# A two-block transformer on one core: each weight unit's high part made by ScalarE in two instructions instead of one

## The chip, the cores and the metric

The kernel runs on one core of a Trainium2 chip, as one program and one launch. The metric is the device time of that program in microseconds, the median of several executions; lower is better. TensorE (PE) multiplies, VectorE (DVE), ScalarE (ACT) and GpSimd (POOL) work on whole tensors in SBUF and PSUM, SyncE (SP) issues the large transfers.

## The reference, cut to what matters

The input is 512 rows of 1024 values, in fp32. They pass through two layers of a first block and one layer of a second, and every matrix product of the reference is to be met at nearly fp32 accuracy.

```python
# first block, two layers
h = rmsnorm(x, g_mix[i])
mix, q_mem = mixer_a(h, ...)      # layer 0: indexer picks 128 keys a row, latent attention
mix, q_mem = mixer_b(h, ...)      # layer 1: causal window attention, window 128, with sinks
mem_o = memory_cross_attention(q_mem, mem_n, w_mem_kv[i])
x = x + concatenate([mix, mem_o]) @ w_out
a, b = split(rmsnorm(x, g_ffn[i]) @ w_up[i])                 # 1024 -> 2 x 2816
x = x + (silu(conv3(a)) * b) @ w_down[i]                     # 2816 -> 1024
# second block, one layer
sh1, sc1, gt1, sh2, sc2, gt2 = split(silu(c) @ w_mod + b_mod, 6)
h = rmsnorm(x, g_pre1) * (1 + sc1) + sh1
q, k, v, f, g_a, g_f = split_proj(h @ w_in)
attn = banded_window_attention_2(q, k, v, k_ctx, v_ctx, sink)
y = (sigmoid(g_a) * (attn @ w_pa) + sigmoid(g_f) * (fourier_mix(f) @ w_pf)) @ w_out
x = x + gt1 * rmsnorm(y, g_post1)
h2 = rmsnorm(x, g_pre2) * (1 + sc2) + sh2
x = x + gt2 * rmsnorm((silu(conv3(u)) * gate) @ w_down, g_post2)   # u, gate from h2 @ w_up
```

## The kernel before, in words

**Weights.** All weight matrices are laid out on the host as 173 units. A unit fills 128 partitions with `ph.size` columns of fp32: 2048 columns in 119 of them, 1408 in 32, 1280 in 16, 1536 in 4, 1024 in 2. The units form one stream of phases (`STREAM`, line 109), and each engine works through it in that order. The phases, with their units: `a_idx` 5, `a_in` 2, `memkv` 4, `a_q` 4, `uk`, `uv`, `a_out` 8 (the first layer's attention and its output), `up00` 22, `dn00` 8, `up01` 22, `dn01` 8 (its feed-forward part in two halves), `b_in` 7, `b_out` 8, `up10`, `dn10`, `up11`, `dn11` (the second layer), `ctx` 2, `c_in` 13, `merge` 4, `c_out` 4, `up20`, `dn200` to `dn203`, `up21`, `dn210` to `dn213` (the second block). The last unit of the program, of `dn213`, has 1536 columns.

**Each unit passes four engines.** SyncE's `load` (line 551) transfers it into one of two slots of `RAW`, which it may overwrite when the low part of the unit two before is written (`sp.wait_ge(lo_ready, ...)`). ScalarE's `hi_unit` (line 602) waits for the transfer and for TensorE to have done with the unit two before, and writes the value rounded to fp32r into a slot of `HI`, the tensor `w_hi` of the trace, in one `ACT.Copy` (line 612). This is called the cast, or the high part. GpSimd's `low` (line 576) waits for the high part and then writes the rest, `raw` minus `w_hi`, into `LO`, the tensor `w_lo`, in pieces of 512 columns (line 582); the last piece signals `lo_ready`. Four pieces are issued for 2048 columns, three for 1408, 1280 and 1536, two for 1024. TensorE waits for `lo_ready` alone, once a unit, then multiplies three times a block, high by high, high by low and low by high: `products` (line 1604) with its matmul in line 1612, `side_by_side` (line 1624, matmul in 1634), in which the first unit after a norm takes the norm's chunks as they come, and `down_rows` (line 2157, matmul in 2167), for the last layer's second feed-forward product. `HI` and `LO` have two slots each too. Counts on the semaphores are multiples of a loop's register where the phase runs in a loop (`each_unit`, line 228), so the number of signals a unit gives is written into the waits.

**The order on ScalarE is written out by hand.** It casts a unit when it comes to it in its program: in the feed-forward phases between its `silu` of two units (`next_hi`), in a norm after the root (`second_unit`, unit 1 of the phase that follows, in `AFTER_NORM`; in `c_in`'s norm between its chunks), in attention between the steps `exps` and `turned`. The sigmoids of the gates (line 992) stand ahead of the casts of `merge`.

**What else is near.** In `dn00`, `dn01` and `dn10` ScalarE issues the transfers of the modulation weights (`load_mod`, issued in line 852) after waiting for VectorE to have used the ones before, and VectorE multiplies them in `mod_unit` (line 1196, product in 1203). In the norms VectorE makes squares (line 1214 as part of `sum_square`, line 1225 the running sum) and `h_lo`, the low part of a chunk of activations (line 1071, or 1067 with a shift), ahead of TensorE. In attention VectorE reduces the scores, adds the sink to the row sums (line 1164) and scales the probabilities (line 1168), which TensorE then transposes (line 1810).

Of the kernel before, what the change touches and what calls it, by code (L numbers as in the profile page):

```python
# [26 lines left out]
ACT = mybir.ActivationFunctionType  # L27
# [3 lines left out]
S = 512  # L31
# [219 lines left out]
def program(nc, wdram, params_d, const_d, axial_d, rows_d, x_d, mem_d, ctx_d, cond_d, pos_d, out_d):  # L251
    ctx = ExitStack()
    with ctx:
        def sem(name):
            return ctx.enter_context(nc.semaphore(name))
# [3 lines left out]
        def at(name, kb, shape, dt=F32):  # L259
            return nc.alloc_sbuf_tensor_at(name, [P] + shape, dt, offset=base + int(kb * KB))  # L260
# [4 lines left out]
        RAW = [at(f"raw{i}", 56 + 8 * i, [2048]) for i in range(2)]  # L265
        HI = [at(f"w_hi{i}", 72 + 8 * i, [2048], F32R) for i in range(2)]
# [80 lines left out]
        for name, n, size, tiles in STREAM:  # L347
            ph = PH[name] = Phase(name, n, size, tiles, land, split)
# [3 lines left out]
        order = [PH[s[0]] for s in STREAM]  # L352
        MOD_PHASES = ["dn00", "dn01", "dn10"]

        raw_landed = [sem("raw_landed0"), sem("raw_landed1")]
        hi_ready, lo_ready = sem("w_hi_ready"), sem("w_lo_ready")

# [214 lines left out]
        @block.gpsimd  # L572
        def _(pool):
            pool.memset(ONES[:], 1.0).then_inc(ones_ready, 1)
            for ph in order:
                def low(i, j, ph=ph):
                    slot = (ph.split + j) % 2

                    pool.wait_ge(hi_ready, 2 * i + (j + ph.split + 1))
                    edges = list(range(0, ph.size, S)) + [ph.size]  # L580
                    for a, z in zip(edges, edges[1:]):
                        ins = nc.gpsimd.tensor_tensor(LO[slot][:, a:z], RAW[slot][:, a:z],  # L582
                                                      HI[slot][:, a:z].bitcast(F32), ALU.subtract)
                    ins.then_inc(lo_ready, 1)
                if ph.name != "a_idx":
                    each_unit(pool, ph.n, low)
                    continue
                for u in range(ph.n):
                    low(u // 2, u % 2)
                    if u != 1:  # L590
                        continue
                    for n, (a, b, some) in enumerate(((0, 2, 1), (4, 6, 2), (0, 4, 2))):
                        pool.wait_ge(x0_squared, some)
                        if n == 2:
                            pool.wait_ge(x0_added, 2)
                        nc.gpsimd.tensor_tensor(XSQ[:, a:a + 2, :], XSQ[:, a:a + 2, :], XSQ[:, b:b + 2, :],
                                                ALU.add).then_inc(x0_added, 1)
# [3 lines left out]
        def _(act):  # L601
            def hi_unit(ph, i, j):

                slot = (ph.split + j) % 2
                act.wait_ge(raw_landed[slot], i * 16 + 16 * ((ph.land + j) // 2 + 1))
                if not isinstance(i, int) or i > 0:
                    act.wait_ge(ph.done, ph.before(2 * i + j - 1))
                elif ph.split + j >= 2:
                    g = ph.split + j - 2
                    q = max((q for q in order if q.split <= g), key=lambda q: q.split)  # L610
                    act.wait_ge(q.done, q.before(g - q.split + 1))
                nc.scalar.activation(HI[slot][:, 0:ph.size], RAW[slot][:, 0:ph.size], ACT.Copy).then_inc(hi_ready, 1)  # L612


            AFTER_NORM = ["up00", "b_in", "up10", "c_in", "up20"]
# [286 lines left out]
            ph = PH["b_in"]  # L902
# [27 lines left out]
            ph = PH["ctx"]  # L930
# [23 lines left out]
            ph = PH["c_in"]  # L954
# [39 lines left out]
            ph = PH["merge"]  # L994
# [1230 lines left out]
```

## Time and profile before

| | |
|---|---|
| median of the runs | 2153.35 us |
| lowest and highest of 3 | 2152.22 and 2154.03 us |
| the profiled execution's own time | 2153.0 us |
| its span | 2151.2 us |
| TensorE busy / GpSimd / ScalarE / VectorE | 94% / 40% / 32% / 51% |
| mean granted clock of TensorE | 0.975 |

The span is the stretch that the trace covers; all positions are microseconds from its start. A row of the groups tells a line's busy time and the mean of one instruction, and after it the idle time of the engine just before these instructions with its releaser. In the timeline the idle time and releaser stand in brackets at the instruction that waited. "PE psum L1612 <- POOL w_lo L582" reads: TensorE's matmul of line 1612, writing `psum`, was released by GpSimd's instruction of line 582, which wrote `w_lo`. Lines on PEld are the weight loads ahead of the matmuls.

### The profile page before, as it was taken

What the parts mean: (1) busy time and instruction counts of PE and PEld (TensorE: products, weight loads), DVE (VectorE), ACT (ScalarE), POOL (GpSimd) and SP (SyncE); (2) the same over time, 40 slices, a digit from 0 to 9 for tenths busy, and PEclk for the clock granted to TensorE, in tenths of its full rate; (3) what the DMA queues carried; (4) which work ended last, traced back from release to release, by engine and by line L of the source; (5) the groups of instructions that cost most, each with busy time, mean ns of one, the idle gap of its engine ahead of it and who ended that gap; (6) DMA issues with size and microseconds to landing.
All of it is one profiled execution on the core that took longest, in us unless ns stands there. A gap on an engine that the chain in (4) does not pass through costs nothing.

```text
span 2151.2 us, 25966 instructions
## 1 busy us (share of the span) xinstructions
PE 2013.4 (94%) x9782; PEld 1614.6 (75%) x9782; DVE 1106.9 (51%) x1998; ACT 680.7 (32%) x1082; POOL 865.6 (40%) x644
## 2 busy tenths in 40 slices
PE   3988789999999989999999999999999989999998
PEld 3766567788778776558788888788876878888886
DVE  7777864533943576764534534872223544322323
ACT  3232463322122134562321222234444333211222
POOL 4343103444744554015445544543221523444442
PEclk9999899999999999999999999999999979999999
DMA  4222001432532341003323422331120212222221
GB/s 160 78 79 98 25 1 62 150 106 84 210 137 91 122 168 59 25 13 112 126 91 139 170 98 93 103 110 67 60 79 1 98 59 79 98 89 98 97 93 74
DMA packets 31634, 199.21 MB, mean 93 GB/s; under 512 B 3632, under 2 KB 3760, under 8 KB 12720
## 3 DMA queue, kind: packets, MB, share of 16 engines
q1 hardware_dynamic: 26640, 166.74, 21.6%
q10 hardware_dynamic: 4896, 31.15, 3.9%
q8 instruction: 64, 1.05, 0.2%
q14 instruction: 34, 0.28, 0.0%
HBM read 195.78 MB, written 2.10 MB: 92 GB/s over the span
## 4 chain that ended last, share of the span: by engine, by line
PE 50%; DVE 3%; POOL 1%; ACT 1%; issue 1%; POOLq 0%; DVEq 0%; ACTq 0%
PE psum L1612 37%; PE psum L2167 5%; PE psum L1634 2%; PE psum L1828 1%; POOL w_lo L582 1%; PE psum L1810 1%; PE psum L1793 1%; PE psum L2095 1%; PE psum L1718 1%; ACT w_hi L612 0%; PE psum L2135 0%; DVE work L1269 0%; DVE h_lo L1067 0%; DVE work L1270 0%; PE psum L2080 0%
## 5 line engine op out<-in xcount | busy, mean ns | idle before, releaser
L582 POOL TENSOR_TENSOR w_lo<-raw,w_hi 128x512 fp32r<-128x512 f32 (+2 forms) x636 | 857.1, 1377 | 1260.7 <-ACT w_hi L612 1260.7
L1612 PE MATMUL psum<-h_hi,w_hi 128*128 128x512 f32 x1560 | 616.8, 395 | 14.1 <-POOL w_lo L582 6.6
L1612 PE MATMUL psum<-h_hi,w_lo 128*128 128x512 f32 x1560 | 610.8, 392 | 0.0
L1612 PE MATMUL psum<-h_lo,w_hi 128*128 128x512 f32 x1560 | 610.2, 391 | 0.0
L612 ACT ACTIVATE w_hi<-raw 128x2048 fp32r<-128x2048 f32 (+3 forms) x173 | 300.8, 1739 | 554.8 <-PE psum L1612 394.9
L1612 PEld LDWEIGHTS psum<-h_hi,w_hi 128*128 128x128 f32 x1560 | 293.8, 188 | 90.8 <-issue 18.4
L1612 PEld LDWEIGHTS psum<-h_hi,w_lo 128*128 128x128 f32 x1560 | 293.9, 188 | 62.6 <-issue 0.7
L1612 PEld LDWEIGHTS psum<-h_lo,w_hi 128*128 128x128 f32 x1560 | 294.1, 188 | 60.4 <-issue 0.8
L1305 DVE TENSOR_SCALAR work<-psum,params 128x512 f32<-128x512 f32 x66 | 53.5, 810 | 222.3 <-PE psum L1612 213.6
L748 ACT ACTIVATE work<-work 128x512 f32<-128x512 f32 x66 | 41.7, 632 | 398.4 <-DVE work L1309 398.4
L1612 PE MATMUL psum<-g_hi,w_hi 128*128 128x512 f32 x352 | 139.1, 395 | 9.2 <-POOL w_lo L582 5.8
L1612 PE MATMUL psum<-g_lo,w_hi 128*128 128x512 f32 x352 | 137.1, 389 | 0.0
L1612 PE MATMUL psum<-g_hi,w_lo 128*128 128x512 f32 x352 | 137.1, 389 | 0.0
L1319 DVE TENSOR_TENSOR work<-psum,work 128x512 f32<-128x512 f32 x66 | 45.6, 692 | 175.0 <-PE psum L1612 170.9
L1203 DVE CUSTOM_DVE_ANT_0 work_flat<-mod_w,conditions 128x1024 f32<-128x1024 f32 x64 | 115.6, 1807 | 1.6
L1309 DVE SCALAR_TENSOR_TENSOR work<-psum,params,work 128x511 f32<-128x511 f32 (+1 forms) x132 | 98.9, 749 | 16.0 <-DVE work L1305 2.2
L1256 DVE TENSOR_TENSOR xT<-psum,xT 128x512 f32<-128x512 f32 (+1 forms) x48 | 33.1, 690 | 132.9 <-PE psum L1612 132.7
L1612 PEld LDWEIGHTS psum<-g_hi,w_hi 128*128 128x128 f32 x352 | 66.1, 188 | 28.7 <-POOL w_lo L582 9.5
L1634 PE MATMUL psum<-h_hi,w_hi 128*128 128x512 f32 x96 | 43.9, 457 | 42.6 <-DVE h_lo L1345 33.1
L1612 PEld LDWEIGHTS psum<-g_hi,w_lo 128*128 128x128 f32 x352 | 66.1, 188 | 14.0
L1612 PEld LDWEIGHTS psum<-g_lo,w_hi 128*128 128x128 f32 x352 | 66.1, 188 | 13.2
L1148 DVE CUSTOM_DVE_ANT_0 work_c<-psum,const 128x512 f32<-128x512 f32 (+1 forms) x32 | 23.0, 755 | 99.5 <-PE psum L1793 99.5
(345 smaller groups left out, 2756.3 us busy)
## 6 DMA issues: line engine op xcount, KB each, us to landing
raw<-w_up SPq DMA_DIRECT2D x66, 1024.0 KB, 4.8
mod_w<-w_mod ACTq DMA_DIRECT2D x24, 1024.0 KB, 4.9
raw<-w_dn SPq DMA_DIRECT2D x32, 704.0 KB, 4.2
raw<-w_c_in SPq DMA_DIRECT2D x13, 1024.0 KB, 4.8
raw<-w_dn SPq DMA_DIRECT2D x8, 1024.0 KB, 4.9
raw<-w_b_in SPq DMA_DIRECT2D x7, 1024.0 KB, 4.8
raw<-w_a_idx SPq DMA_DIRECT2D x5, 1024.0 KB, 5.6
raw<-w_a_out SPq DMA_DIRECT2D x8, 640.0 KB, 3.8
```

What stands on the lines that cost most here:

```text
L582: ins = nc.gpsimd.tensor_tensor(LO[slot][:, a:z], RAW[slot][:, a:z], HI[slot][:, a:z].bitcast(F32), ALU.subtract)
L612: nc.scalar.activation(HI[slot][:, 0:ph.size], RAW[slot][:, 0:ph.size], ACT.Copy).then_inc(hi_ready, 1)
L748: nc.scalar.activation(T[:, 2 + j, :], T[:, j, :], ACT.Silu).then_inc(silu_ready, 1)
L1148: ins = nc.vector.tensor_tensor_reduce(probs_of(s, n), src, st["mask"], 1.0, -PICKED, ALU.add, ALU.min, o[:, n:n + 1])
L1203: ins = nc.vector.tensor_tensor_reduce(TW[:, 4 * S:4 * S + D], MODW[u % 2][:, c, :], COND[:, w, :], 1.0, 0.0, ALU.mult, ALU.add, MODV[:, 2 ...
L1256: nc.vector.tensor_tensor(d, bank(j), d, ALU.add).then_inc(ph.free, 1)
L1305: step(nc.vector.tensor_scalar(t, a, w(mid), w(3), ALU.mult, ALU.add))
L1309: ins = nc.vector.scalar_tensor_tensor(out=t[:, o], in0=a[:, s_], scalar=w(k), in1=t[:, o], op0=ALU.mult, op1=ALU.add)
L1319: nc.vector.tensor_tensor(g, b, T[:, 2 + j, :], ALU.mult).then_inc(ph.free, 1)
L1612: ins = nc.tensor.matmul(out, l, r, start=(k == 0 and m == 0), stop=(k == n - 1 and m == 2))
L1634: ins = nc.tensor.matmul(out, w, a, start=(k == 0 and m == 0), stop=(k == kc - 1 and m == 2))
L2167: ins = nc.tensor.matmul(bank(4 * f + t), a[:, k, g], b[slot][:, w], start=k == 0 and m == 0, stop=k == HALF - 1 and m == 2)
```

## The change

`hi_unit` writes the high part in two instructions instead of one, cut at `hi_cut(ph)`: 1024 columns for units of 2048, 1536, 1408 and 1280, and 512 for units of 1024. Each of the two signals `hi_ready`, so a unit gives two signals where it gave one. `low` waits for the first signal ahead of its first piece and for the second one ahead of the piece that begins at the cut; pieces, their number and `lo_ready` stay as they are. The multiples in the waits are doubled to match. Nothing else is touched: neither the place of `hi_unit` in ScalarE's program, nor its waits, nor TensorE's.

```diff
--- before.py
+++ after.py
@@ -352,6 +352,10 @@
         order = [PH[s[0]] for s in STREAM]
         MOD_PHASES = ["dn00", "dn01", "dn10"]
 
+        def hi_cut(ph):
+
+            return S * ((-(-ph.size // S) + 1) // 2)
+
         raw_landed = [sem("raw_landed0"), sem("raw_landed1")]
         hi_ready, lo_ready = sem("w_hi_ready"), sem("w_lo_ready")
 
@@ -576,9 +580,12 @@
                 def low(i, j, ph=ph):
                     slot = (ph.split + j) % 2
 
-                    pool.wait_ge(hi_ready, 2 * i + (j + ph.split + 1))
                     edges = list(range(0, ph.size, S)) + [ph.size]
                     for a, z in zip(edges, edges[1:]):
+                        if a == 0:
+                            pool.wait_ge(hi_ready, 4 * i + (2 * (j + ph.split) + 1))
+                        if a == hi_cut(ph):
+                            pool.wait_ge(hi_ready, 4 * i + (2 * (j + ph.split) + 2))
                         ins = nc.gpsimd.tensor_tensor(LO[slot][:, a:z], RAW[slot][:, a:z],
                                                       HI[slot][:, a:z].bitcast(F32), ALU.subtract)
                     ins.then_inc(lo_ready, 1)
@@ -609,7 +616,8 @@
                     g = ph.split + j - 2
                     q = max((q for q in order if q.split <= g), key=lambda q: q.split)
                     act.wait_ge(q.done, q.before(g - q.split + 1))
-                nc.scalar.activation(HI[slot][:, 0:ph.size], RAW[slot][:, 0:ph.size], ACT.Copy).then_inc(hi_ready, 1)
+                for a, z in ((0, hi_cut(ph)), (hi_cut(ph), ph.size)):
+                    nc.scalar.activation(HI[slot][:, a:z], RAW[slot][:, a:z], ACT.Copy).then_inc(hi_ready, 1)
 
 
             AFTER_NORM = ["up00", "b_in", "up10", "c_in", "up20"]
```

## Rows read from the trace of the kernel before

**Rows 1.** The page: busy us, share of the span and instructions of each engine.

```profile
PE 2013.4 (94%) x9782; PEld 1614.6 (75%) x9782; DVE 1106.9 (51%) x1998; ACT 680.7 (32%) x1082; POOL 865.6 (40%) x644
```

**Rows 2.** Waits, whole span: engine, line, releaser, us in total, times, longest.

```profile
PEld psum L1612 <- POOL w_lo L582: 19.3, 14, 4.0
...
PE psum L1612 <- POOL w_lo L582: 12.4, 8, 3.6
```

**Rows 3.** Groups by shape: count, busy us, mean ns, idle before them.

```profile
L612 ACT ACTIVATE w_hi<-raw 128x2048 fp32r<-128x2048 f32 x119 | 228.1, 1917 | 284.2 <-PE psum L1612 187.9 <-PE psum L2167 40.7 <-PE psum L1634 38.2
...
L582 POOL TENSOR_TENSOR w_lo<-raw,w_hi 128x512 fp32r<-128x512 f32 x588 | 799.8, 1389 | 1260.7 <-ACT w_hi L612 1260.7
```

**Rows 4.** Timeline, a unit of 1024 columns: start us, us, engine, line.

```profile
1387.54 1.06 ACT L612 ACTIVATE w_hi<-raw 128x1024 fp32r<-128x1024 f32 x1 [4.24 <-PE psum L1612]
1388.67 2.99 POOL L582 TENSOR_TENSOR w_lo<-raw,w_hi 128x512 fp32r<-128x512 f32 x2 [0.83 <-ACT w_hi L612]
```

**Rows 5.** Timeline of PE and its weight loads: where they waited for `w_lo`.

```profile
597.25 0.50 PE L1612 MATMUL psum<-h_hi,w_hi 128*128 128x512 f32 x1 [3.57 <-POOL w_lo L582]
1210.39 0.50 PE L1612 MATMUL psum<-h_hi,w_hi 128*128 128x512 f32 x1 [0.65 <-POOL w_lo L582]
1371.05 0.50 PE L1612 MATMUL psum<-g_hi,w_hi 128*128 128x512 f32 x1 [1.07 <-POOL w_lo L582]
1667.58 0.50 PE L1612 MATMUL psum<-h_hi,w_hi 128*128 128x512 f32 x1 [2.38 <-POOL w_lo L582]
1700.69 0.19 PEld L1634 LDWEIGHTS psum<-m_hi,w_hi 128*128 128x128 f32 x1 [0.57 <-POOL w_lo L582]
2126.98 0.50 PE L2167 MATMUL psum<-w_hi,g_hi 128*128 128x512 f32 x1 [2.72 <-POOL w_lo L582]
```

**Rows 6.** Timeline, end of the first modulation stretch, into `up01` unit 1.

```profile
600.75 0.08 DVE L1203 DVE_READ_ACCUMULATOR2_ANT mod<- 128x1 f32 x1
604.10 5.05 POOL L582 TENSOR_TENSOR w_lo<-raw,w_hi 128x512 fp32r<-128x512 f32 x4 [6.90 <-ACT w_hi L612]
609.88 0.39 PE L1612 MATMUL psum<-h_hi,w_hi 128*128 128x512 f32 x1
```

**Rows 7.** Timeline, the port stage at `up11` unit 0: VectorE and GpSimd.

```profile
1204.23 1.23 DVE L1203 CUSTOM_DVE_ANT_0 work_flat<-mod_w,conditions 128x1024 f32<-128x1024 f32 x1
1204.35 5.99 POOL L582 TENSOR_TENSOR w_lo<-raw,w_hi 128x512 fp32r<-128x512 f32 x4 [3.29 <-ACT w_hi L612]
```

**Rows 8.** Timeline, `dn11` unit 5: VectorE and GpSimd.

```profile
1366.05 0.69 DVE L1225 TENSOR_TENSOR work<-work 128x512 f32<-128x512 f32 x1
1366.54 4.46 POOL L582 TENSOR_TENSOR w_lo<-raw,w_hi 128x512 fp32r<-128x512 f32 x3 [5.55 <-ACT w_hi L612]
```

**Rows 9.** Timeline, second block's attention: `L1168` without and beside a low part.

```profile
848.22 0.62 DVE L1168 TENSOR_SCALAR work_flat<-work_flat,stats 128x256 f32<-128x256 f32 x2
854.73 5.03 POOL L582 TENSOR_TENSOR w_lo<-raw,w_hi 128x512 fp32r<-128x512 f32 x4 [20.49 <-ACT w_hi L612]
857.52 2.39 DVE L1168 TENSOR_SCALAR work_flat<-work_flat,stats 128x256 f32<-128x256 f32 x2
859.96 0.33 PE L1810 MATMUL psum<-const,work_flat 128*128 128x128 f32 x1 [3.49 <-DVE work_flat L1168]
```

**Rows 10.** Timeline of VectorE in two norms, with and without GpSimd busy.

```profile
781.98 1.18 DVE L1214 TENSOR_TENSOR work<-xT 128x512 f32<-128x512 f32 x1
1019.03 0.69 DVE L1214 TENSOR_TENSOR work<-xT 128x512 f32<-128x512 f32 x1
1024.82 1.22 DVE L1071 TENSOR_TENSOR h_lo<-work,h_hi 128x512 fp32r<-128x512 f32 x1
1030.12 0.68 DVE L1071 TENSOR_TENSOR h_lo<-work,h_hi 128x512 fp32r<-128x512 f32 x1
```

**Rows 11.** Windows: us, then PE, PEld, DVE, ACT, POOL busy (x), PEclk, DMA.

```profile
598.50:601.50 3.00, 3.00 (x8) 2.31 (x8) 2.29 (x4) 0.00 (x0) 0.00 (x0) 0.50 0.82 314
...
1668.00:1672.00 4.00, 4.00 (x19) 3.28 (x18) 1.83 (x3) 3.52 (x3) 1.00 (x1) 1.00 0.68 262
```

## Prediction

> **What bounds the kernel now.** I read the page's first rows: TensorE is busy 94% of the span, GpSimd 40%, ScalarE 32% [rows 1]. Nothing that ScalarE or GpSimd does can matter unless TensorE waits for it, so the second view is the table of waits. It charges GpSimd with 1260.7 us of idle time ahead of `w_lo`, which looks like the prize and is not: that is a slow-loaded engine waiting for work [rows 3]. What counts is the other direction. TensorE waited for `w_lo` 12.4 us in eight places, beside the one of `L2167` below, and its weight loads 19.3 us in fourteen [rows 2]; the loads' figure holds the same stalls again, plus short waits in which the load idled and the multiplication hardly did. Third, the timeline at those places [rows 5] and just ahead of them, to see what the low part itself had been waiting for. Fourth, TensorE's other idle time: where VectorE was late, was GpSimd working beside it? That view turned out to carry as much as the first.
>
> **How far a low part moves.** A high part of 1024 columns takes 1.06 us, and the low part starts 1.13 us after it began, so the handoff is 0.07 us [rows 4]. One of 2048 columns takes 1917 ns [rows 3], so its low part now starts about 1.99 us after the high part. After the change it starts when the first 1024 columns are done, at 1.13 us: 0.86 us sooner. The two lengths give 0.84 ns a column, so a unit of 1280, 1408 or 1536 columns, cut at 1024 too, gains 0.21, 0.32 or 0.43 us. A unit of 2048 is 119 of the 173. The second half ends at about 2.1 us, while the first two pieces of 1.25 us each (a quarter of 5.05 [rows 6]) keep GpSimd until 3.6 us: the added wait never holds anything up, and nobody waits behind it on GpSimd's queue but the pieces themselves. The transfer into `raw` is released by `lo_ready`, so it only starts earlier.
>
> **What ScalarE pays.** Two instructions of 1.06 us instead of one of 1.92 add at most 0.21 us a unit, 36 us over 173 units, on an engine that has 68% of the span free. It lies on TensorE's path only where ScalarE's next instruction is what TensorE waits for. Unit 1 of `c_in` is cast between the chunks of the norm before it; there I count 0.2 us. Elsewhere the work behind the cast waits for TensorE or VectorE longer than that. No row shows a wait that is already satisfied between two GpSimd pieces. From above I bound it by the handoff, 0.07 us a unit [rows 4], from below by nothing; I take nothing, because a satisfied wait has nothing to hand over.
>
> **The direct stalls, one by one** [rows 5].
> - 1667.58, idle 2.38 us, `merge` unit 1: the high part stood behind ScalarE's sigmoids, nothing else shifts. Gain 0.86.
> - 2126.98, idle 2.72 us, the last unit, 1536 columns, VectorE silent. Gain 0.43.
> - 597.25, idle 3.57 us, `up01` unit 0. Before it lies a stretch in which VectorE's weight products (`L1203`) and GpSimd's pieces slow each other, and several casts wait behind `load_mod` for VectorE, whose last product ends at 600.75. That end is the sum of both engines' work and won't move. The low part of unit 1 ends at 609.15 and TensorE reaches it at 609.88 [rows 6], so the whole stretch, with its two other stalls, can give back no more than 0.86 + 0.73 = 1.6 us, whatever happens inside. I take 0.86.
> - 1210.39, idle 0.65 us, `up11` unit 0. The low part reached GpSimd at 1204.35, when a product had just started, took 5.99 instead of about 5.05, and was held by it for the difference [rows 7]. Arriving 0.86 sooner it goes ahead of that product but then meets it later. Between 0 and 0.65; I take 0.4.
> - 1371.05, idle 1.07 us, and two like it at 1379 and 1388 (`dn11`). The low part arrived at 1366.54 inside `L1225`, which runs 1366.05 to 1366.74 [rows 8]. 0.32 us sooner is 1366.22, inside the same instruction, so if it holds the port the first piece starts when it did. Between 0 and 3 x 0.32; I take 0, since all three look alike.
> - The short ones, such as 1700.69 with 0.57: 0.5 us for all six together, between 0 and 1.
>
> Direct: 0.86 + 0.43 + 0.86 + 0.4 + 0.5 = 3.05 us.
>
> **The indirect stalls.** In the second block's attention `L1168`, two short instructions that read one tensor in SBUF, take 0.62 us, but 2.39 beside a low part; TensorE then idled 3.49 us. The low part ran 854.73 to 859.78, undelayed, and `L1168` ended as its last piece did [rows 9]. So VectorE is released by the end of the burst, and the burst ends 0.86 us sooner. ScalarE's added 0.2 us doesn't matter there, since what follows waits for the pieces. Three stalls have this form (833, 860 and 891 us), two smaller ones belong to units of 1280 columns (325 and 920): 3 x 0.83 + 2 x 0.2 = 2.9. In the norm before `b_in`, `L1214` took 1.18 us beside the tail of a low part, and 0.69 in another norm [rows 10]; that tail now ends before it: 0.4.
> Here a rule of the Trainium skill bears on the change. Its page "GPSIMD Engine Reference", section "Specifications", says that GpSimd shares its SBUF interfaces with VectorE and contends with VectorE instructions in a two-port mode or with two SBUF inputs. The trace agrees, with `L1168` at 2.39 us against 0.62. Taken alone the rule speaks against counting on any start that moves beside VectorE's work, and would leave only 1667.58 and 2126.98 of the sum, 2152.1 us.
> The same contention can turn against the change. `L1071`, the first `h_lo` of a norm, took 1.22 us beside a low part, 0.68 alone [rows 10]. Four norms and `c_in`'s have such a first chunk, on TensorE's path; moving the pieces by 0.86 us puts some in front of it and takes others away, by at most 0.9 each. I read two as worse and two as better: 0, between -2 and +2.
>
> **The sum.** 3.05 + 2.9 + 0.4 - 0.2 = 6.15 us. The profiled execution took 2153.0 us, 0.35 below the median of 2153.35, so the rows are typical. Forecast 2153.35 - 6.15 = 2147.2, a fall of 0.29%. A measurement here can tell about 0.2%, 4.3 us, from no change.
>
> **Rivals.**
> 1. The clock comes back too. After the stall of 597.25 TensorE's granted clock was 0.50 for some 3 us, its lower level of 1.2 GHz: 8 multiplications in 3.00 us, against 18 weight loads in 4.00 us after 1667.58 at 1.00 [rows 11]. Each such fall costs about 1.6 us of dense work. It followed idle times of 3.57, 3.49 and 2.72 us and not 2.38. If shorter stalls avert two to four falls (there are five beside stalls of this kind), 2141 to 2144. For it: 2.72 becomes 2.3. Against: one of the five followed a stall of 1.7 only. 17%.
> 2. The port eats the gain. Indirect stalls end when VectorE's order says so, not when the burst ends, and stalls beside VectorE stay: 6.15 less 2.9, 0.4 and 1.3, about 2151, within 2149.1 to 2153.9. 26%.
> 3. Slower. The mechanism is GpSimd going ahead of a VectorE instruction on TensorE's path, a full piece (1.25 us) a time. Places: the norms above and `L1164`/`L1168` in the third block's attention, where eleven casts fall and TensorE now waits hardly ever. To pass +4.3 it takes (6.15 + 4.3) / 1.25, nine net collisions: about 2159. Against it, that attention's VectorE is mostly idle. 5%.
> 4. It doesn't do what it says: the pieces don't start at the first signal, or the added wait empties GpSimd's queue at a cost like the handoff's, and ScalarE's 36 us show where casts queue: 2153 to 2156, 5%.
> My forecast, 2144 to 2149: 47%.
>
> **How the numbers follow.** Faster by over 0.2%, under 2149.04: the forecast and rival 1, 64%. Within: rival 2 and most of 4, 30%. Slower: 6%. For 8 in 10 the range must hold the forecast, rival 2 and the nearer half of rival 1: 2142 to 2153.
>
> **What would show it.** Low parts of 2048 columns start 1.13 us after their cast; casts in pairs of 1.06 us; 636 pieces as before. 1667.58's idle 2.38 becomes 1.5, 2126.98's 2.72 becomes 2.3, the three of 3.5, 3.5 and 1.7 in the attention lose 0.8 each, and the `dn11` ones stay. `up01` unit 1 begins 0.9 to 1.6 us sooner after the end of `dn00` than it does now. Wrong if the attention's stalls keep their length, if TensorE shows new waits for VectorE, or if the spells at 0.50 change in number: each is worth 1.6 us, as much as two of my terms.

## The result, and the profile after

The changed kernel takes 2138.5 us, the median of four runs (2137.65 to 2142.02), where the kernel before takes 2153.5: a ratio of 0.9937 with a 95% interval of 0.9923 to 0.9951, and 0.9941 (0.9928 to 0.9954) when it was run again. The fall is 13 to 15 us, more than twice the 6.15 us that was forecast, and it lies outside the range of 2142 to 2153. The first trace of the changed kernel spans 2135.8 us, 15.4 less than the one of before.

The page's first row of the changed kernel:

```profile
PE 2005.2 (94%) x9782; PEld 1609.2 (75%) x9782; DVE 1164.7 (55%) x1998; ACT 696.2 (33%) x1255; POOL 895.7 (42%) x644
```

Its waits for `w_lo` (L1620 is L1612 of before, L1642 is L1634, L2175 is L2167, L589 is L582, L1176 is L1168):

```profile
PEld psum L1620 <- POOL w_lo L589: 14.6, 12, 3.4
PE psum L1620 <- POOL w_lo L589: 10.1, 13, 3.0
PE psum L2175 <- POOL w_lo L589: 2.3, 1, 2.3
```

Two things are to be seen. TensorE's waits for `w_lo` at `products` fell by only 2.3 us [rows 2], and by 2.7 us with that of the last unit (2.7 to 2.3), far less than 15. And TensorE was busy for 8.2 us less with the same 9782 multiplications [rows 1]: they ran faster, which no wait explains. GpSimd (865.6 to 895.7) and VectorE (1106.9 to 1164.7) were busy longer with the same instructions. Most of VectorE's part is `g_lo`, 66 instructions that took 46 us and now take 99, and no idle time of TensorE grew behind them. In two other places, at 833 us and in the norm before `c_in`, the change does cost TensorE an idle time; they are named below.

The stalls that the prediction named, in the timeline of the changed kernel, answering to [rows 5] and [rows 9]:

```profile
592.13 0.50 PE L1620 MATMUL psum<-h_hi,w_hi 128*128 128x512 f32 x1 [2.97 <-POOL w_lo L589]
...
851.09 0.33 PE L1818 MATMUL psum<-const,work_flat 128*128 128x128 f32 x1 [2.62 <-DVE work_flat L1176]
...
1199.12 0.50 PE L1620 MATMUL psum<-h_hi,w_hi 128*128 128x512 f32 x1 [0.37 <-POOL w_lo L589]
...
1359.66 0.50 PE L1620 MATMUL psum<-g_hi,w_hi 128*128 128x512 f32 x1 [0.96 <-POOL w_lo L589]
...
1654.88 0.50 PE L1620 MATMUL psum<-h_hi,w_hi 128*128 128x512 f32 x1 [1.09 <-POOL w_lo L589]
...
2113.21 0.50 PE L2175 MATMUL psum<-w_hi,g_hi 128*128 128x512 f32 x1 [2.30 <-POOL w_lo L589]
```

And the handoff at `merge`, in the kernel before and then in the changed one:

```profile
1659.66 1.90 ACT L612 ACTIVATE w_hi<-raw 128x2048 fp32r<-128x2048 f32 x1
1661.64 5.88 POOL L582 TENSOR_TENSOR w_lo<-raw,w_hi 128x512 fp32r<-128x512 f32 x4 [58.56 <-ACT w_hi L612]
```

```profile
1648.23 1.99 ACT L620 ACTIVATE w_hi<-raw 128x1024 fp32r<-128x1024 f32 x2
1649.35 5.47 POOL L589 TENSOR_TENSOR w_lo<-raw,w_hi 128x512 fp32r<-128x512 f32 x4 [58.67 <-ACT w_hi L620]
```

The low part starts 1.12 us after the start of the cast instead of 1.98, as worked out. The pair of casts takes 1.99 us, against 1.90 for the one cast at this place before: the split costs ScalarE 0.09 us here. Over the span ScalarE is busy 15.5 us longer, 0.09 a unit; the prediction had 0.21 as the most that it could be.

**Where the 15.4 us lie.** TensorE executes the same 9782 instructions in the same order in both kernels, so the start of the nth can be compared with the start of the nth. The lead grows by 7.1 us where an idle time is shorter, by 0.9 us where a weight load is, and by 7.4 us in stretches where one of the two traces shows the granted clock at 0.50, 1.2 GHz, and the other at 1.00; such a stretch at 0.50 is called a spell. The trace of before has sixteen spells, that of after twelve. One that left and one that stayed, in the changed kernel's windows (their counterparts in before both stand at 0.50, from 861 and from 892 us):

```profile
852.00:855.40 3.40, 3.40 (x28) 2.08 (x22) 2.71 (x14) 2.23 (x8) 0.00 (x0) 1.00 0.48 185
880.60:884.00 3.40, 3.40 (x14) 2.05 (x10) 1.98 (x10) 1.90 (x7) 0.00 (x0) 0.50 0.48 182
```

The columns are those of [rows 11]: both follow an idle time of 2.6 us and do similar work, 28 multiplications at the one clock and 14 at the other.

### The profile page after: what moved, and what is told of

It is laid out like the page before. It is cut to its first block, busy times and chain, and to the rows that moved or that the text cites. A ratio compares the mean times of both kernels' runs of the same rounds, so it can differ in the third digit from the quotient of the medians.

```text
span 2135.8 us, 26221 instructions
## 1 busy us (share of the span) xinstructions
PE 2005.2 (94%) x9782; PEld 1609.2 (75%) x9782; DVE 1164.7 (55%) x1998; ACT 696.2 (33%) x1255; POOL 895.7 (42%) x644
## 4 chain that ended last, share of the span: by engine, by line
PE 51%; DVE 2%; ACT 1%; POOL 1%; issue 1%; POOLq 0%; DVEq 0%; ACTq 0%
PE psum L1620 38%; PE psum L2175 6%; PE psum L1642 2%; PE psum L1836 2%; PE psum L1818 1%; PE psum L1801 1%; POOL w_lo L589 1%; PE psum L2103 1%; PE psum L1726 1%; ACT w_hi L620 0%; PE psum L2143 0%; DVE work L1277 0%; DVE work L1278 0%; PE psum L2088 0%; PE psum L1764 0%
## 5 line engine op out<-in xcount | busy, mean ns | idle before, releaser
L589 POOL TENSOR_TENSOR w_lo<-raw,w_hi 128x512 fp32r<-128x512 f32 (+2 forms) x636 | 887.5, 1424 | 1216.8 <-ACT w_hi L620 1216.8
L1620 PE MATMUL psum<-h_hi,w_hi 128*128 128x512 f32 x1560 | 615.7, 395 | 11.9 <-POOL w_lo L589 5.3
L1620 PE MATMUL psum<-h_hi,w_lo 128*128 128x512 f32 x1560 | 609.3, 391 | 0.0
L1620 PE MATMUL psum<-h_lo,w_hi 128*128 128x512 f32 x1560 | 609.0, 390 | 0.0
L620 ACT ACTIVATE w_hi<-raw 128x1024 fp32r<-128x1024 f32 (+1 forms) x346 | 316.5, 964 | 549.1 <-PE psum L1620 372.0
L1620 PEld LDWEIGHTS psum<-h_hi,w_hi 128*128 128x128 f32 x1560 | 293.0, 188 | 89.1 <-issue 20.0
L1620 PEld LDWEIGHTS psum<-h_hi,w_lo 128*128 128x128 f32 x1560 | 293.1, 188 | 62.6 <-issue 0.7
L1620 PEld LDWEIGHTS psum<-h_lo,w_hi 128*128 128x128 f32 x1560 | 293.2, 188 | 59.7 <-issue 0.8
L1620 PE MATMUL psum<-g_hi,w_hi 128*128 128x512 f32 x352 | 138.7, 394 | 8.2 <-POOL w_lo L589 4.8
L1620 PE MATMUL psum<-g_lo,w_hi 128*128 128x512 f32 x352 | 137.1, 389 | 0.0
L1620 PE MATMUL psum<-g_hi,w_lo 128*128 128x512 f32 x352 | 137.1, 389 | 0.0
L1330 DVE TENSOR_TENSOR g_lo<-work,g_hi 128x512 f32 (+1 forms) x66 | 98.9, 1498 | 6.5
L1264 DVE TENSOR_TENSOR xT<-psum,xT 128x512 f32<-128x512 f32 (+1 forms) x48 | 33.1, 690 | 126.4 <-PE psum L1620 126.1
L1620 PEld LDWEIGHTS psum<-g_hi,w_hi 128*128 128x128 f32 x352 | 66.0, 188 | 27.1 <-POOL w_lo L589 7.7
L1642 PE MATMUL psum<-h_hi,w_hi 128*128 128x512 f32 x96 | 43.2, 450 | 41.3 <-DVE h_lo L1353 32.5
L1620 PEld LDWEIGHTS psum<-g_hi,w_lo 128*128 128x128 f32 x352 | 66.1, 188 | 14.0
```

Source lines behind the costliest of these rows:

```text
L620: nc.scalar.activation(HI[slot][:, a:z], RAW[slot][:, a:z], ACT.Copy).then_inc(hi_ready, 1)
L1330: nc.vector.tensor_tensor(chunk(GL), g, chunk(GH).bitcast(F32), ALU.subtract).then_inc(g_ready, 1)
L1620: ins = nc.tensor.matmul(out, l, r, start=(k == 0 and m == 0), stop=(k == n - 1 and m == 2))
L1642: ins = nc.tensor.matmul(out, w, a, start=(k == 0 and m == 0), stop=(k == kc - 1 and m == 2))
```

## The experiments

Spans below are of single traces; medians are of all runs. Two executions of one kernel differ by up to 2.7 us ahead of 330 us, mostly by spells of the clock, so stretches behind that are compared.

**Was it the earlier start, and was it the placement of two traces?** Both kernels once more, and one in which GpSimd waits for the second cast:

```diff
                     for a, z in zip(edges, edges[1:]):
                         if a == 0:
-                            pool.wait_ge(hi_ready, 4 * i + (2 * (j + ph.split) + 1))
-                        if a == hi_cut(ph):
                             pool.wait_ge(hi_ready, 4 * i + (2 * (j + ph.split) + 2))
```

> ScalarE makes the high part in the same two instructions, but GpSimd waits for the second one before its first piece, so that the low part starts about 2.17 us after the cast instead of 1.13 (before: 1.99). Theory H (head start): everything came from the earlier start, and it is gone; the longer cast delays the low parts by 0.2 us, which costs about 0.2/0.86 of the 8 us of waits, 1.9 us, and some clock: 2153 to 2157 us. Rival T (re-timing): the gain is that everything on ScalarE and GpSimd was shifted against VectorE and against the clock's spells, in whatever direction; then this kernel, shifted too, gains as well: 2140 to 2148 us.

Measured: 2154.74 us, ratio to before 1.0022 (1.0012 to 1.0031). Theory H. The gain is gone, and the two-piece cast with nothing in return costs 3.5 to 5 us by the medians; its trace is of a run 2.7 us below the median and doesn't show where. At `merge` and in the last unit the stalls came back, longer by the 0.09 us of the second cast (L618 is L620 of the changed kernel, L587 is L589):

```profile
1658.22 1.99 ACT L618 ACTIVATE w_hi<-raw 128x1024 fp32r<-128x1024 f32 x2
1660.29 5.89 POOL L587 TENSOR_TENSOR w_lo<-raw,w_hi 128x512 fp32r<-128x512 f32 x4 [58.86 <-ACT w_hi L618]
1666.23 0.50 PE L1618 MATMUL psum<-h_hi,w_hi 128*128 128x512 f32 x1 [2.47 <-POOL w_lo L587]
2126.10 0.54 PE L2173 MATMUL psum<-w_hi,g_hi 128*128 128x512 f32 x1 [2.81 <-POOL w_lo L587]
```

Not every stall did. That of 3.57 us came back as 3.36, and the first of `dn11`, 1.07 us before, is 0.30 here with no head start at all: shifted against VectorE, a stall can shrink too. Rival T is thus true of single places and not of the whole. And its trace had no spell behind the stalls at 595 and 830 us, which are 3.36 and 1.81 us long: spells can leave without much help from shorter stalls.

> The kernel before, once more, for a second trace and the clock of each run. Of the 15.4 us that the span fell, an instruction-by-instruction comparison of TensorE in the two traces puts 7.1 us on shorter idle times, 0.9 on weight loads, and 7.4 on spells at granted clock 0.50 (16 of them before, 12 after). Theory P (placement): the spells belong to the stalls, so a second trace of the kernel before shows the same spells at 598, 834, 861 and 2127 us, and the whole 7.4 us is the change's. Rival C (chance): where a spell falls depends on how a stall happens to lie in time, so that a second trace shows other ones, two or more of those four missing or new ones elsewhere, with 1.5 us each; then a part of the 7.4 us is luck of the two traces, and the runs of one kernel spread by 2 to 4 us.

> The changed kernel, once more. Both theories: idle times as in its first trace within 0.1 us a place, ratio 0.993. Theory P: the same 12 spells, runs within 1.5 us of 2138. Rival C: spells at other places, for instance back at 598 or 2115 us, gone at 952, and runs from 2137 to 2143. If P holds on both kernels, the clock's share is a part of the mechanism; if C holds on both, the mean of the runs says what it is worth.

Measured: before 2151.97 us (pooled with the other runs beside it 2151.2), after 2137.85. The second trace of before, 2.7 us ahead by then, has the spells at 598, 834, 861, 892 and 2127 us at the same instructions, within 0.1 us; the second trace of after lacks four of them again and has the new one at 952 again. That is theory P for the stalls in question. Elsewhere it is rival C: before has fourteen spells in its second trace and not sixteen, those at 291 and 1407 us are gone, after has ten and not twelve, and after's runs go up to 2140.42 us, where P allowed 1.5 us around 2138. And a kernel that repeats itself says nothing on whether a shorter stall or another position did it.

**Length or position of the stalls.** In both kernels the first multiplication of unit 1 of `up00`, `b_in`, `up10`, `c_in` and `up20` is issued N times more, N = 3, 5, 10 and 13, so that all stalls behind 420 us move and none of the six below changes:

```diff
+                        while k == 0 and m == 0 and again[0]:
+                            again[0] -= 1
+                            nc.tensor.matmul(out, l, r, start=True, stop=True)
                         ins = nc.tensor.matmul(out, l, r, start=(k == 0 and m == 0), stop=(k == n - 1 and m == 2))
```

> The kernel before, with the first multiplication of unit 1 of up00, b_in, up10, c_in and up20 issued five times more (start and stop set, so that it is overwritten): 5 x 5 x 0.227 = 5.7 us of dense TensorE work in all, 1.13 us at each place, and every stall behind one of them comes 1.13 us later with its length unchanged. What is open is why spells of the clock at 0.50 left the changed kernel. Theory L (length): a spell follows a long stall, and the changed kernel lost them because its stalls are shorter; then this kernel keeps the spells at 598, 834, 861, 891 and 2127 us and takes before + 5.7 us, within 1. Rival P (placement): whether a spell follows depends on where in time a stall falls, as 2.97 us without a spell in the changed kernel and 2.98 us with one in quarters suggest; then two or more of those five are gone or new ones appear, and the time is before + 5.7 us, changed by 1.6 us for each.

> The changed kernel with the same five more at each place. L: none of 598, 834, 861 and 2127 comes back, 891 (880.6 in its trace) stays, after + 5.7 us. P: some come back, in other places, and the gain over before_5more differs from 13 us by 1.6 us for each. The idle times themselves are as in the changed kernel, so over before_5more the waits give 6 to 8 us by both.

> The same with ten more at each place, 2.27 us each and 11.3 us in all. L: the same five spells, before + 11.3 us. P: another set than in before and in before_5more. Over the kernel before and these two, the count of these five spells tells how often a stall of such a length has one: 5 of 5 each time by L, some other share by P.

> The changed kernel with ten more at each place. As after_5more: by L after + 11.3 us with the same spells, by P another set. The mean over the three placements (0, 5, 10) of the difference between before and after is what the change is worth with the luck of placement taken out: by L 13 us, by P nearer to the waits alone, 8 to 10 us.

> The kernel before with three more multiplications at each of the five places: 0.68 us each, 3.4 us in all. So far, over the placements 0, 5 and 10, the six stalls at 598, 834, 861, 892, 961 and 2127 us had 5, 3 and 4 spells of the clock in the kernel before, 2, 3 and 5 in the changed one; 861 had one in all of before and none of after, 961 the reverse. Theory L2 (mostly placement): here 3 to 5 of the six, 861 among them, 961 not.

> The changed kernel with the same three more. L2: 2 to 5 of the six stalls have spells, 861 not, 961 yes; the difference to before_3more lies between 8.7 and 13.1 us. Theory L (the change averts spells for good): 2 of the six, and a difference of 13 us.

> The same with thirteen more, 2.95 us each and 14.7 us in all: a fifth placement. L2 as for before_3more.

> The changed kernel with thirteen more. With this the mean difference over five placements (0, 3, 5, 10, 13) stands: by L2 it is 10 to 11.5 us, of which some 8 to 9 are shorter waits, and the 13 us of the unshifted kernels hold about 2 us of luck; by L it is 13.

Measured, medians in us, and how many of the six stalls (at 597, 833, 860, 891, 964 and 2127 us of before) had a spell behind them; for N = 0 the runs and traces of `before_again` and `after_again`:

| N | before | after | difference | spells before | spells after |
|---|---|---|---|---|---|
| 0 | 2151.97 | 2137.85 | 14.1 | 5 | 2 |
| 3 | 2154.41 | 2139.03 | 15.4 | 5 | 2 |
| 5 | 2154.63 | 2145.93 | 8.7 | 3 | 3 |
| 10 | 2166.48 | 2154.94 | 11.5 | 3 | 5 |
| 13 | 2166.74 | 2155.80 | 10.9 | 4 | 3 |
| mean | | | 12.1 | 4.0 | 3.0 |

The same stall, unchanged in length, with and without a spell; the changed kernel at N = 0 and N = 5, then before at N = 10:

```profile
592.60:596.00 3.40, 3.40 (x17) 2.79 (x16) 3.30 (x7) 0.00 (x0) 0.00 (x0) 1.00 0.72 260
```

```profile
597.10:600.30 3.20, 3.20 (x9) 2.43 (x9) 3.10 (x7) 0.00 (x0) 0.00 (x0) 0.50 0.90 289
```

```profile
600.00:603.40 3.40, 3.40 (x16) 2.80 (x16) 2.98 (x6) 0.00 (x0) 0.00 (x0) 1.00 0.84 279
```

The idle times ahead of these are 2.97, 2.94 and 3.56 us; before at N = 0 had 3.57 and a spell [rows 5, 11]. So neither theory holds alone. Position seems to decide in the single case; this rests on one trace for each shifted kernel, and on the two traces each at N = 0, which agree in all six places. Length bears on how often: the two stalls of 3.5 us in the attention (861 and 892) had a spell in 10 of 10 cases, and in both of `both_wait`; shortened to 2.6 us, in 5 of 10. The others show little: 4 of 5 at 3.57 and 3 of 5 at 2.95 us; 3 of 5 at 2.72 and 2 of 5 at 2.30; 2 of 5 both at 1.72 and at 2.12; the stall of 1.52 us, which the change does not touch, 1 of 5 and 3 of 5.

The forecasts of single places failed: at N = 3 the stall of 1.52 us had a spell in the kernel before and none in the changed one, and 861 had one in the changed one, all three against what was expected. So did the range for the difference at N = 3, 8.7 to 13.1 us (measured 15.4). The mean of 12.1 us lies between the 10 to 11.5 and the 13 of the two theories, and with the spread of the five differences it is uncertain by some 3 us either way, so it decides for neither; what speaks against pure length are the spells that came and went. Nor are the six all there is of the clock: before at N = 10 has two fewer of them than at N = 0 and is yet 3 us slower than the work added.

The Trainium skill says in "TensorE: Matmul & The Clock Gate", section "Part 1: The HAM clock gate (the "warmup" mystery)", that the gate's view of activity runs free and does not restart with the kernel, so that one kernel can meet it in different ways. The traces agree in part: the spells of before at 291 and 1407 us are missing in its second trace, the five behind the stalls are not.

**Which stalls end with the burst?** Pieces of 256 columns in `b_in` alone, and the change in `b_in` alone:

```diff
-                    edges = list(range(0, ph.size, S)) + [ph.size]
+                    step = S // 2 if ph.name == "b_in" else S
+                    edges = list(range(0, ph.size, step)) + [ph.size]
```

> The changed kernel, but in the seven units of b_in GpSimd writes the low part in pieces of 256 columns, eight a unit, instead of four of 512. It tells how L1176 (L1168 of before), two instructions on VectorE, is held up. My prediction took it that VectorE is released by the end of the burst (theory E): then the idle times at 851 and 880 us stay at 2.6 us or grow, since eight pieces take longer (some 5.3 us instead of 5.0). Rival G (gaps between pieces): a VectorE instruction gets in at the end of a piece, one a piece, so 2.39 us is two pieces; then L1176 takes about 2 x 0.65 = 1.3 us, L1172 is held less too, and both idle times fall by 1 to 1.3 us: ratio to the changed kernel 0.999.

Measured: ratio to before 0.9932 (0.9919 to 0.9946), no clear difference from the change in the medians; of the spells behind the six stalls that at 952 left, one came in the last unit, and that behind 880 gave way to one behind 851. The idle times tell. First the changed kernel, GpSimd and VectorE ahead of 851.09, then this one:

```profile
845.87 5.02 POOL L589 TENSOR_TENSOR w_lo<-raw,w_hi 128x512 fp32r<-128x512 f32 x4 [19.36 <-ACT w_hi L620]
848.65 2.39 DVE L1176 TENSOR_SCALAR work_flat<-work_flat,stats 128x256 f32<-128x256 f32 x2
```

```profile
845.67 6.09 POOL L590 TENSOR_TENSOR w_lo<-raw,w_hi 128x256 fp32r<-128x256 f32 x8 [17.75 <-ACT w_hi L621]
848.73 1.31 DVE L1177 TENSOR_SCALAR work_flat<-work_flat,stats 128x256 f32<-128x256 f32 x2
850.10 0.44 PE L1819 MATMUL psum<-const,work_flat 128*128 128x128 f32 x2 [1.83 <-DVE work_flat L1177]
```

The burst became longer (6.09 us, against 5.02) and VectorE's pair shorter, 1.31 instead of 2.39 us; TensorE's idle times went from 2.62 to 1.83, twice, and from 2.13 to 0.64 at 829 us, 0.8 us where rival G had 1 to 1.3. TensorE went on at 850.10 us while the burst ran until 851.76, so theory E is out. Rival G: each VectorE instruction that reads as `L1176` does is held to the end of the piece under way, so two cost two pieces. It explains why 833 got worse with the change. In the kernel before:

```profile
829.26 4.97 POOL L582 TENSOR_TENSOR w_lo<-raw,w_hi 128x512 fp32r<-128x512 f32 x4 [6.21 <-ACT w_hi L612]
830.81 2.27 DVE L1168 TENSOR_SCALAR work_flat<-work_flat,stats 128x128 f32<-128x128 f32 x2
```

And in the changed one:

```profile
821.52 4.99 POOL L589 TENSOR_TENSOR w_lo<-raw,w_hi 128x512 fp32r<-128x512 f32 x4 [6.07 <-ACT w_hi L620]
822.05 0.79 DVE L1164 SCALAR_TENSOR_TENSOR stats<-params,stats 128x2 f32<-128x2 f32 x1
823.56 0.52 DVE L1172 TENSOR_TENSOR stats<-stats 128x2 f32<-128x2 f32 x1 [0.72 <-ACT stats L710]
824.32 2.27 DVE L1176 TENSOR_SCALAR work_flat<-work_flat,stats 128x128 f32<-128x128 f32 x2
```

The burst of before ended at 834.23 and `L1168` was done at 833.08, with the third piece. After the change the pieces start earlier against VectorE and catch two more of its instructions (`L1164` 0.79 us and `L1172` 0.52, instead of 0.16 and 0.22); `L1176`, again 2.27 us, ends with the fourth. The rule stands in the Trainium skill's page "SBUF — State Buffer", section "Who interferes with whom": where a VectorE instruction in a two-port mode meets GpSimd, whoever issues first has the shared ports for the whole instruction, and the other blocks. The trace agrees, with 2.39 and 1.31 us.

> The high part in two instructions, with the early start of the low part, in the seven units of b_in alone (the second layer's attention); all other units as in the kernel before. Between 850 and 950 us each of the three placements gave 3.4 to 3.5 us to the changed kernel (two idle times 3.49 to 2.63, one 1.28 to 1.08, and one spell of the clock fewer), and lost 1.6 behind it to a spell at the idle time of 1.52 ahead of b_out, and 0.4 at 833 us. Theory A (local): all of that belongs to b_in's units and shows here unchanged; the norm ahead of b_in, whose 1.0 us came from the last unit of dn01, does not; ratio 0.9993, 2150 us where before has 2151.5. Rival B (carried): the spell at the idle time of 1.52 depends on how the kernel comes out of the stretches before, and the 3.45 or the 1.6 are different here; a gain of 3 us or none.

Measured: 2146.29 us, ratio 0.9978 (0.9969 to 0.9987), some 4 us where 1.5 were forecast. The trace is of the slowest of its eleven runs, 2151.07 us, 4.8 above the median, so it can't be used for the whole. Against the second trace of before, the stretch from 850 to 950 us gave 3.2 us (idle times 3.49 to 2.62, twice, and one spell fewer) and 833 lost 0.4, as in the full change; this is local. But the spell at the idle time of 1.52 did not come, and the one behind 892 left while that behind 861 stayed, the reverse of the full change. So theory A holds for the waits and rival B for the clock. The stretch accounts for 2.8 of the 4 us; what the rest is stays open.

**Further along the same way.** Four casts a unit, each signalled, with each of GpSimd's pieces waiting for its own; and then two edits where a low part was still late: ScalarE casts unit 1 of `merge` ahead of the sigmoids, and VectorE writes the low part of the last unit, which GpSimd leaves out.

```diff
-                        if a == 0:
-                            pool.wait_ge(hi_ready, 4 * i + (2 * (j + ph.split) + 1))
-                        if a == hi_cut(ph):
-                            pool.wait_ge(hi_ready, 4 * i + (2 * (j + ph.split) + 2))
+                        pool.wait_ge(hi_ready, 8 * i + (4 * (j + ph.split) + 1 + a // S))
...
-                for a, z in ((0, hi_cut(ph)), (hi_cut(ph), ph.size)):
-                    nc.scalar.activation(HI[slot][:, a:z], RAW[slot][:, a:z], ACT.Copy).then_inc(hi_ready, 1)
+                edges = list(range(0, ph.size, S)) + [ph.size]
+                for a, z in zip(edges, edges[1:]):
+                    nc.scalar.activation(HI[slot][:, a:z], RAW[slot][:, a:z], ACT.Copy).then_inc(
+                        hi_ready, 1 if z < ph.size else 6 - len(edges) + 0)
```

> ScalarE makes the high part in pieces of 512 columns, each signalled, and each of GpSimd's pieces waits for its own. The low part starts 0.63 + 0.07 = 0.70 us after the cast, 0.43 sooner than in the changed kernel; the cast of 2048 columns takes 4 x 0.63 = 2.5 us instead of 2.1. Theory H: direct stalls that begin with ScalarE (1654.9, the last unit, the attention's) lose another 0.4 us each, in all about 0.43/0.86 of the first 8 us where nothing else bounds, so 2 to 4 us: 2134 to 2137 us. Rival S (ScalarE or VectorE takes over): units behind a norm and the sigmoids pay the longer cast, and the rest of the stalls ends with VectorE: 2138 to 2141 us, no better than the change.

Measured: 2136.34 us, ratio 0.9933 (0.9921 to 0.9945); the intervals of this and of the change overlap, so the times alone don't tell theory H from rival S. By the traces `merge` (1.09 to 0.69) and the last unit (2.30 to 1.89) gained their 0.4 us, the attention's pair 0.2 each.

```diff
             ph = PH["merge"]
+            next_hi(ph, 0, 0)
             gates(0)
...
+                        for a in (0, S, 2 * S):
+                            v.wait_ge(hi_ready, 4 * g + 1 + a // S)
+                            ins = nc.vector.tensor_tensor(LO[g % 2][:, a:a + S], RAW[g % 2][:, a:a + S],
+                                                          HI[g % 2][:, a:a + S].bitcast(F32), ALU.subtract)
+                        ins.then_inc(lo_ready, 1)
```

> Quarters with two edits at the places where a low part was still late: ScalarE casts unit 1 of merge ahead of the sigmoids instead of behind them, and VectorE, idle there, writes the low part of the last unit in three pieces of 0.69 us, while GpSimd skips it. Theory H: the idle time at merge, 0.69 us in quarters, goes to 0; that at the last unit, 1.89 us, goes to about 0.1: 2.4 us less than quarters, 2134 us. Rival: the later sigmoids (2 us) make VectorE's products with the gates late, and TensorE waits for m_lo in c_out instead; and a spell more or less, 1.6 us each, hides it: 2135 to 2138.

Measured: 2132.04 us, ratio 0.9916 (0.9902 to 0.9929), as theory H had it and somewhat better; its interval still touches that of `quarters`. The wait at `merge` is gone and that of the last unit is 0.06 us; VectorE writes that low part in less than two us where GpSimd took 3.7:

```profile
2106.18 1.89 DVE L1592 TENSOR_TENSOR w_lo<-raw,w_hi 128x512 fp32r<-128x512 f32 x3 [4.88 <-ACT w_hi L620]
```

> Quarters_plus with the low part of b_in's seven units in pieces of 256 columns. In b_pieces_256 this took 1.5 us from the idle time at 829 us and 0.8 from each of those at 854 and 882: 3.0 us less than quarters_plus, 2129 us, if the spells of the clock stay (1.6 us for each that goes or comes). If the pieces gained there only because of the two-piece cast, the idle times stay at 1.9 and 2.4 us and the time at 2132.

Measured: 2131.01 us, ratio 0.9903 (0.9886 to 0.9920), where 2129 was expected; the intervals of this and of `quarters_plus` overlap, so it is not shown to be faster. The idle times fell by 0.99 (1.92 to 0.93) and by 0.34 twice (2.43 to 2.1), little more than half of the 3 us expected. Why the two fell so little here stays open.

## Why the prediction was wrong

**The step that failed is the sum's silence on the clock.** It put nothing for TensorE's spells at 0.50 and left them to a rival of 17%, on top of the waits, of which the range held only the nearer half. The four fewer spells of that rival came, and more waits than summed as well: in the first pair 8.0 us of idle times and loads against 6.15, and 7.4 us of clock against 0. The waits alone would have given some 2145 us, inside the range; even the rival's lower end, 2141, was too high. In five placements, from 549 us on, the waits and loads are worth 5.6 (mean of two pairs), 7.6, 10.0, 5.3 and 4.8 us, mean 6.7, and the clock 5.5, 2.6, -2.9, 4.2 and 2.3, mean 2.3. How a stretch divides between the two is uncertain where a stall lies inside a spell; the sums aren't. The traces of after happen to be of runs 1.7 to 3 us above their kernels' medians (2140.3 beside 2137.85, 2148.5 beside 2145.9), which is most of what is missing to 12.1. So the change is worth about 12 us, give or take 3, with the luck of position taken out: some 8 us of waits (with those ahead of 549 us, below), and some 4 us by subtraction. The granted clock of all runs says the same of the 4: what is missing to full clock, (1 - granted clock) x span, is 52.0 us in the mean run of before and 46.2 in that of after at N = 0, and over the five placements after has 4.1 us less. This is an estimate, and at most what the clock gave, since a spell in an idle time costs nothing. Of the 7.4 us of clock between the first two traces 2.1 lie ahead of 549 us, where the second pair has -3.6, and 5.3 behind it, where the mean is 2.3: several us that another position would not give.

**Point by point.**
- Start of the low part, 0.86 us sooner: right, 1.12 us after the cast.
- ScalarE's cost: 0.09 us a unit, within the bound of 0.21. `both_wait` shows that it matters where the low part follows it.
- The 0.2 us set aside for it in the norm before `c_in`: the first pair hides the place, since both traces have a spell there. In the second pair, and in the others in which TensorE waits there, the idle time went from 1.00 to 1.37 us. In `both_wait`, with the longer cast alone, it is 1.08. The rest is `L1075` (L1067 of before), which took 1.27 us and now takes 1.56 beside a low part that starts sooner. So the place costs 0.4, of which ScalarE's share is 0.1. From `before_again` and `after_again`:

```profile
1408.63 0.50 PE L1634 MATMUL psum<-h_hi,w_hi 128*128 128x512 f32 x1 [1.00 <-DVE h_lo L1067]
1403.78 0.50 PE L1642 MATMUL psum<-h_hi,w_hi 128*128 128x512 f32 x1 [1.37 <-DVE h_lo L1075]
```

- 1667.58: forecast 0.86, measured 1.29. GpSimd's pieces also took 5.47 instead of 5.88 us; that they met VectorE's products otherwise is likely, not shown.
- 2126.98: forecast 0.43, measured 0.42. 1210.39: 0.4, measured 0.28. `dn11`: 0, measured 0.11 at the first and nothing at the two others. The short ones at 1700: about 0.4. Not in the list: the starts of six units of `dn01`, 734 to 774 us, where the first multiplications are drawn out behind late weight loads; five gave 0.1 to 0.3 us each and one lost 0.3. From 622 to 783 us the lead grew by 0.8 to 1.0 in every pair.
- The stretch up to 610 us: bounded at 1.6, taken as 0.86, measured 1.37 in the first pair. Inside it three stalls went down by 1.3, 1.3 and 0.6 us, four others came with 0.4 to 0.8, and a spell left, and all of it gave 1.4 together. A bound on the whole was the right tool, since the single stalls would have misled. But at other positions the stretch gave 0.9 to 2.5, past the bound at N = 10 (1.9) and N = 13 (2.5), where before has a longer spell at 581 and at 598 us: the bound left out the clock.
- The indirect stalls: 2.9 forecast, 1.75 measured as idle time: 0.87 and 0.86 at 860 and 891, 0.2 and 0.2 at the two small ones, but minus 0.40 at 833. The step "VectorE is released by the end of the burst" failed; it was read from one case in which the last piece's end and the burst's end are the same. It is the end of a piece.
- The norm before `b_in`: 0.4 forecast. Its `L1222` (L1214 of before) did take 0.90 instead of 1.18 us, but TensorE's idle time behind it stayed, 1.31 after 1.28, so the term gave nothing there.
- The norms, taken as 0 within -2 and +2: one gave 0.7 to 1.0. At 1773 us `L1067`, the first chunk's `h_lo`, took 1.79 us beside a low part, and after the change 0.93, beside one that starts sooner; the idle time of 0.99 behind it is gone. Others lost, by less: the same instruction in the norm at 1025 us took 1.23 us and then 1.41 in the second pair, that at 789 us 1.42 and then 1.62. The norm at 1773, before and after:

```profile
1773.06 1.79 DVE L1067 SCALAR_TENSOR_TENSOR h_lo<-work,mod,h_hi 128x512 fp32r<-128x512 f32 x1
1774.99 0.47 PE L1634 MATMUL psum<-h_hi,w_hi 128*128 128x512 f32 x1 [0.99 <-DVE h_lo L1067]
```

```profile
1760.80 0.93 DVE L1075 SCALAR_TENSOR_TENSOR h_lo<-work,mod,h_hi 128x512 fp32r<-128x512 f32 x1
1761.87 0.76 PE L1642 MATMUL psum<-h_hi,w_hi 128*128 128x512 f32 x1
```

- Not in the list at all: the very first unit. TensorE's first multiplication began at 33.1 to 33.5 us in six traces of before and its shifted forms, and at 32.4 to 32.6 in those of the change, 0.8 us, the head start once more. The idle time of 2.84 us at 132 became 2.61.

**The rivals.** The slower case had no sign. "It doesn't do what it says" is excluded by the handoff of 1.12 us. "The port eats the gain" is true of one stall of five. Its price is off by a little: 6.15 less 2.9, 0.4 and 1.3 leaves 1.55, so 2151.8 and not about 2151. The first rival was right in kind: of the five spells it named, four were absent from the first trace, and two to four of them were its condition.

## What to carry to other kernels

Splitting a producer's instruction so that its consumer follows the first half gains the half at every handoff that is exposed; in this kernel, with TensorE at 94%, the exposed ones are few, and each must be found by its idle time, the very first one and those in which VectorE stands between included. A change that shortens several idle times of 2.5 to 3.5 us should carry a term for the clock in its sum, as an expected number of spells times 1.5 us with a wide range, and a difference of two kernels below some 3 us should be looked at in more than one position before it is put down to a mechanism. Where GpSimd and VectorE both read SBUF, count VectorE's instructions against the pieces of GpSimd: each costs up to a piece, so that shorter pieces beside a critical VectorE chain can shorten the wait even if the burst gets longer (2.62 to 1.83 us here, with a burst of 6.09 instead of 5.02).

## What the runs showed of the hardware

- A spell of TensorE's clock at 0.50 costs 1.5 to 1.6 us of dense work. Behind an idle time of 3.5 us in the attention there was one in 10 of 10 cases, behind 2.6 us in 5 of 10, and between traces in which a stall of unchanged length lay 0.7 us or more elsewhere it came or went.
- Two executions of the kernel before, 2.7 us apart after 330 us, showed the five spells behind its stalls at the same instructions, and differed in others. Why a kernel falls into step like this is open; so is whether the spell at the unchanged idle time of 1.52 us is commoner after the change (3 of 5, against 1 of 5) by more than chance.
- Instructions as small as 128x2 on VectorE take longer beside a GpSimd piece too: `L1164` of the kernel before took 1.25 us beside one, at 856 us, and 0.15 alone, at 851.
